# Down product of a gated FFN: five places for raw operands in place of three, and three work lists reordered

## What is computed

```
h = rms_norm(x, norm_ffn)
up = causal_dwconv(h @ ffn_w_up, ffn_conv_w, ffn_conv_b)        # 2048 x 5632, three taps
u_val, u_gate = split(up, 2)
x = x + (gelu(u_gate) * u_val) @ ffn_w_down                     # 2816 -> 1024
out = rms_norm(x, norm_final)
```

## Time and profile before

| | us |
|---|---|
| median of 3 runs (lowest, highest) | 2575.82 (2570.79, 2579.19) |
| the profiled execution | 2580.78 |
| its span in the trace | 2579.0 |
| down product of half 0, first matmul to first matmul of what follows three uses later | 1664.55 to 1912.53 |
| down product of half 1 | 2341.34 to 2560.31 |
| TensorE busy | 2435.2 (94%) |

### The profile page before, as it was taken

How to read it: one execution, slowest core, us unless ns; L and a number is a source line. 1 busy time by engine, 2 the same in 40 slices (tenths; PEclk the granted TensorE clock), 3 DMA queues, 4 the chain that set the end, 5 groups by cost and what they waited for, 6 DMA issues and landing times.

```text
span 2579.0 us, 33398 instructions
## 1 busy us (share of the span) xinstructions
PE 2435.2 (94%) x11968; PEld 1952.1 (76%) x11968; DVE 1707.7 (66%) x2323; ACT 1129.5 (44%) x2008; POOL 978.5 (38%) x784
## 2 busy tenths in 40 slices
PE   7999999999799996997899999999899999998997
PEld 5777777777677775775688888777678788787886
DVE  7554447775255675351787887767778888886755
ACT  6434254332146554321544444443564444444444
POOL 4111003432055772221555555333235556551310
PEclk9999999899899998998899999999999999999999
DMA  4233324442497424544332332386542322326764
GB/s 163 98 98 103 100 74 152 142 150 93 157 312 247 129 63 163 178 157 172 151 116 100 114 116 98 119 277 225 188 155 95 119 102 106 119 90 211 234 193 161
DMA packets 189444, 376.60 MB, mean 146 GB/s; under 512 B 17104, under 2 KB 61152, under 8 KB 180192
## 3 DMA queue, kind: packets, MB, share of 16 engines
q1 hardware_dynamic: 189280, 374.47, 42.7%
HBM read 250.43 MB, written 123.98 MB: 145 GB/s over the span
## 4 chain that ended last, share of the span: by engine, by line
PE 38%; DVE 7%; issue 2%; DMA 2%; ACT 2%; POOL 1%; SPq 0%; ACTq 0%; DVEq 0%; POOLq 0%
PE ff_bank L2107 13%; PE ff_bank L2109 12%; PE ff_bank L2108 12%; DVE ff_ring L2817 2%; DVE ff_y_gate L2804 2%; DMA ff_raw_ring<-t_t 1%; DVE ff_ring L2765 1%; DVE ff_b_lo L2759 1%; ACT ff_y_gate L2619 1%; DMA ff_raw_ring<-a_t 0%; ACT ff_ring L2634 0%; DMA ff_b_raw<-h_t 0%; DVE ff_u L2786 0%; ACT ff_e L2598 0%; DVE ff_u L2788 0%
## 5 line engine op out<-in xcount | busy, mean ns | idle before, releaser
L2107 PE MATMUL ff_bank<-ff_b_hi,ff_ring 128*128 128x512 f32 x1232 | 486.6, 395 | 29.7 <-DVE ff_b_lo L2759 13.0
L2108 PE MATMUL ff_bank<-ff_b_lo,ff_ring 128*128 128x512 f32 x1232 | 482.3, 392 | 0.0
L2109 PE MATMUL ff_bank<-ff_b_hi,ff_ring 128*128 128x512 f32 x1232 | 482.2, 391 | 0.0
L2817 DVE TENSOR_TENSOR ff_ring<-ff_raw_ring,ff_ring 128x512 fp32r<-128x512 f32 x308 | 240.2, 827 | 132.9 <-ACT ff_ring L2634 132.8
L66 PE MATMUL ip_bank<-ip_x_hi,ip_w_hi 128*128 128x512 f32 x736 | 306.1, 416 | 20.0 <-DVE ip_x_lo L701 16.8
L2107 PEld LDWEIGHTS ff_bank<-ff_b_hi,ff_ring 128*128 128x128 f32 x1232 | 232.8, 189 | 93.7 <-issue 43.2
L67 PE MATMUL ip_bank<-ip_x_lo,ip_w_hi 128*128 128x512 f32 x736 | 296.8, 403 | 0.0
L68 PE MATMUL ip_bank<-ip_x_hi,ip_w_lo 128*128 128x512 f32 x736 | 295.9, 402 | 0.0
L2107 PE MATMUL ff_bank<-ff_ring 128*128 128x512 f32 x616 | 245.2, 398 | 27.5 <-DVE ff_ring L2817 23.4
L2109 PEld LDWEIGHTS ff_bank<-ff_b_hi,ff_ring 128*128 128x128 f32 x1232 | 232.9, 189 | 49.2
L2108 PEld LDWEIGHTS ff_bank<-ff_b_lo,ff_ring 128*128 128x128 f32 x1232 | 233.1, 189 | 47.8 <-issue 0.5
(11 more groups left out here) (263 smaller groups left out, 4618.4 us busy)
## 6 DMA issues: line engine op xcount, KB each, us to landing
ff_raw<-in_slabs SPq DMA_DIRECT2D x43, 1024.0 KB, 4.8
proj_t<-ip_staged SPq DMA_DIRECT2D x92, 256.0 KB, 2.7
a_t<-ff_y_val SPq DMA_DIRECT2D x44, 512.0 KB, 2.6
t_t<-ff_t_sum SPq DMA_DIRECT2D x88, 256.0 KB, 2.0
ff_raw_ring<-s_t SPq DMA_DIRECT2D x88, 256.0 KB, 3.2
ff_raw_ring<-t_t SPq DMA_DIRECT2D x88, 256.0 KB, 3.8
ff_raw_ring<-in_w_down SPq DMA_DIRECT2D x66, 256.0 KB, 3.1
ff_raw_ring<-a_t SPq DMA_DIRECT2D x66, 256.0 KB, 4.4
```

What stands on the lines that cost most here:

```text
L2107: pe.matmul(out, w_hi, x_hi, start=first, stop=False, skip_group_check=resumed)
L2108: pe.matmul(out, w_hi, x_lo, start=False, stop=False, skip_group_check=resumed)
L2109: return pe.matmul(out, w_lo, x_hi, start=False, stop=last, skip_group_check=resumed)
L2817: dve.tensor_tensor(ring[:, to, 1, :], raw_ring[:, raw_slot(half, n), i, :], ring[:, to, 0, :].bitcast(F32), ALU.subtract).then_inc(d_lo_r ...
```

## The change

Two more raw places, `spare`, are put over `b_hi[6]`. Steps take places by n mod 5; in half 0 only up to step 64, from step 65 they take the old three again, and `high_b` of B11 waits until the low parts of step 64 are made. A load waits for the low parts of the last step that had its place; loads 3 and 4 wait for the end of the half's up product, since they go where `b_hi[6]` was. Lists: on SyncE the last stores go from behind load 8 to behind load 10, `load_x` to behind 14 to 29, `load_piece` to behind 30 to 45. On ScalarE high step 3 goes ahead of the last tap; squares go to 56 to 59 and 62 to 65, `high_b` starts at 48. On VectorE low step 3 goes ahead of the last convolution and low step 4 between it and the gating; `norm_b` comes one per step from 36 to 51. On GpSimd the last four totals of half 0 go ahead of the sums of the next slab.

```diff
+        spare = placed("spare", [P, 2, 2, KH * P], 6 * KH * NB * 4)
-        d_in = [sem(f"d_in{i}") for i in range(3)]
+        d_in = [sem(f"d_in{i}") for i in range(5)]
+        RAW_FIVE = 65
-        def raw_slot(half, n):
-            return slot(half, n % 3)
+        def raw_number(half, n):
+            return n % 5 if half or n < RAW_FIVE else (n - RAW_FIVE) % 3
+        def raw_at(half, n, i):
+            r = raw_number(half, n)
+            return raw_ring[:, slot(half, r), i, :] if r < 3 else spare[:, r - 3, i, :]
+        def raw_before(half, n):
+            return [m for m in range(n) if raw_number(half, m) == raw_number(half, n)][-1]
...
-                if n >= 3:
-                    sp.wait_ge(d_lo_ready, 2 * (N - 2))
-                else:
-                    sp.wait_ge(product_done, USES * half + 146)
+                if n >= 5:
+                    sp.wait_ge(d_lo_ready, 2 * (STEPS * half + raw_before(half, n) + 1))
+                else:
+                    sp.wait_ge(product_done, USES * half + (146 if n < 3 else USES))
...
-                    if n == 8:
+                    if n == 10:
                         store_a(half, PAIRS - 1)
                         store_t(half, PAIRS - 1)
-                    if 10 <= n < 26:
-                        load_x(half, n - 10)
-                    if half == 0 and 26 <= n < 42:
-                        load_piece(1, n - 26)
+                    if 14 <= n < 30:
+                        load_x(half, n - 14)
+                    if half == 0 and 30 <= n < 46:
+                        load_piece(1, n - 30)
...
                 totals(half, range(OC, 3 * OC))
                 if half == 0:
+                    totals(half, range(3 * OC, 4 * OC))
                     last_sum_of_slab(1, 0)
                     sums_of_slab(1, 1)
-                if half == 0:
-                    totals(half, range(3 * OC, 4 * OC))
...
+                    if o == B11:
+                        act.wait_ge(d_lo_ready, 2 * RAW_FIVE)
...
                 high_step(half, 2)
+                high_step(half, 3)
                 tap(half, PAIRS - 1, 0)
-                for n in range(3, STEPS):
+                for n in range(4, STEPS):
-                    if 44 <= n < 48:
-                        square(half, n - 44)
-                    if 60 <= n < 64:
-                        square(half, n - 60 + OC)
+                    if 56 <= n < 60:
+                        square(half, n - 56)
+                    if 62 <= n < 66:
+                        square(half, n - 62 + OC)
...
-                    if half == 0 and 46 <= n < 46 + 28:
-                        high_b(1, n - 46)
+                    if half == 0 and 48 <= n < 48 + 28:
+                        high_b(1, n - 48)
...
                 low_step(half, 2)
+                low_step(half, 3)
                 convolve(half, PAIRS - 1, 0)
+                low_step(half, 4)
                 multiply(half, PAIRS - 1)
-                for n in range(3, STEPS):
+                for n in range(5, STEPS):
-                    if half == 0 and 33 <= n < 49 and n % 4 == 1:
-                        for i in range(4):
-                            norm_b(n - 33 + i)
+                    if half == 0 and 36 <= n < 52:
+                        norm_b(n - 36)
```

More of the change, by code:

```diff
@@ L2264, in loads_of @@
         def loads_of(half, n):
-            return n // 3 + 1 + half * len(range(n % 3, STEPS, 3))
+            r = raw_number(half, n)
+            return len([0 for h in range(half + 1) for m in range(STEPS if h < half else n + 1) if raw_number(h, m) == r])
         def down_count(half, n, o):
@@ L2354, in load_step @@
                     w = s_t[i, :, SUM_AT[weights], :]
-                sp.dma_start(raw_ring[:, raw_slot(half, n), 1, :], w).then_inc(d_in[n % 3], 16)
+                sp.dma_start(raw_at(half, n, 1), w).then_inc(d_in[raw_number(half, n)], 16)
                 if acts[0] == "B":
@@ L2363, in load_step @@
                     a = t_t[t, i, :, half * NB:(half + 1) * NB]
-                sp.dma_start(raw_ring[:, raw_slot(half, n), 0, :], a).then_inc(d_in[n % 3], 16)
+                sp.dma_start(raw_at(half, n, 0), a).then_inc(d_in[raw_number(half, n)], 16)
             def load_x(half, i):
@@ L2627, in high_step @@
                 N = STEPS * half + n
-                act.wait_ge(d_in[n % 3], 32 * loads_of(half, n))
+                act.wait_ge(d_in[raw_number(half, n)], 32 * loads_of(half, n))
                 if n >= 4:
@@ L2633, in high_step @@
                 for i, to in enumerate((act_slot(half, n), weight_slot(half, n))):
-                    act.activation(ring[:, to, 0, :], raw_ring[:, raw_slot(half, n), i, :], ACT.Copy).then_inc(d_hi_ready, 1)
+                    act.activation(ring[:, to, 0, :], raw_at(half, n, i), ACT.Copy).then_inc(d_hi_ready, 1)
             def keep_first_product(half):
@@ L2816, in low_step @@
                     dve.wait_ge(d_hi_ready, 2 * N + i + 1)
-                    dve.tensor_tensor(ring[:, to, 1, :], raw_ring[:, raw_slot(half, n), i, :], ring[:, to, 0, :].bitcast(F32),
+                    dve.tensor_tensor(ring[:, to, 1, :], raw_at(half, n, i), ring[:, to, 0, :].bitcast(F32),
                                       ALU.subtract).then_inc(d_lo_ready, 1)
```

## The result

| | before | changed |
|---|---|---|
| median (lowest to highest), 4 runs each | 2574.38 (2570.79 to 2579.19) | 2543.75 (2540.20 to 2549.77) |
| ratio, 95% interval | | 0.9877 (0.9859 to 0.9895) |
| the profiled execution | 2580.78 | 2542.92 |
| first down matmul of half 0 | 1664.55 | 1656.60 |
| half 0, to the last matmul before the squares' sum | 248.0 | 226.4 |

30.6 us came off the median; 35.7 were forecast. Between the two profiled executions lie 37.9 us, but 8.0 of them stand ahead of the first down matmul, where nothing was changed.

A forecast was written before the change was run, and what follows sets the result against it. TensorE, kept waiting in places, was taken to bound the kernel. Gains 9.6 + 4.35 + 16.3 + 5.5 = 35.7 us brought the profiled 2580.8 to 2545.1, or 2540.1 us for a median; range 2529 to 2559.

The forecast's parts named there:

- A, the head: Start of both halves' down products: earlier high and low steps remove most of the wait at step 3; 9.6 us gained.
- B, the copy: First product's copy, both halves: loads 11 to 14 go out ahead of the store wait, no wait left; 4.35 us gained.
- C, the middle: Middle of half 0: later squares free ScalarE, norms are spread; 5.0 us of loss left, 16.3 us gained.
- D, the border: Border of half 0 to half 1: earlier totals cut the squares' sum wait from 5.3 to 1.5 us; 5.5 us gained.
- the two bounds: At the head, load 3's activation block lands 3.1 or 4.9 us after it goes out.
- The rival of late loads: Load 3 lands 6 us after issue, TensorE waits at steps 3 to 5, A gives nothing; 2550 us, chance 0.08.
- The lag sum: Middle of half 0: VectorE's lag from norms, sums, drain and `low_b` stalls TensorE 3.9 us at step 52 or 53.
- The dearer price in the prediction: Middle of half 0: each GpSimd sum costs VectorE its full length less idle time, near 1.3 us; 3 us more stall.

The follow-up runs named there:

- lists alone: The changed kernel with the old three raw places instead of five, its reordered lists kept; 2561.0 us, ratio to before 0.9940.
- the memsets: The changed kernel with GpSimd's sixteen sums of normed operands replaced by memsets of the same tiles; 2541.4 us, one run.
- the norms at 33: The changed kernel with VectorE's norms one per step from 33 to 48 instead of 36 to 51; 2543.5 us, ratio to before 0.9855.
- the squares at 50: The changed kernel with the first four squares before high steps 50 to 53 instead of 56 to 59; 2553.0 us, one run.
- the totals late: GpSimd's last four totals behind the slab sums, as before the change; the changed kernel with only this undone took 2542.4 us.
- the old order at the head: The changed kernel with high step 3 and low steps 3 and 4 back behind tap, convolution and gating; 2555.7 us, ratio to before 0.9919.
- the slab sum first: The changed kernel with GpSimd's last sum of slab (1, 0) ahead of the last four totals; 2548.9 us.

## Why the prediction was right

The four terms, in us of the stages, from the tables above:

| term | forecast | measured |
|---|---|---|
| A, the head | 9.6 | 8.7 |
| B, the copy | 4.35 | 4.6 |
| C, the middle | 16.3 | 14.8 |
| D, the border | 5.5 | 1.9 |
| all stages | 35.7 | 29.9 |

**A, the head: 9.6 us forecast, 8.7 measured** (12.9 us lost before, 4.2 after; undoing the order alone costs 8.5). Load 3 landed within the two bounds (1657.17 to about 1661.1 us, 3.9 against 3.1 to 4.9). The stall came in three small pieces a half, not two, without a clock drop: 1.0 and 1.2 us idle, 2.0 and 2.2 us lost against the 1.8 forecast. The rival of late loads is out.

**B, the copy: 4.35 forecast, all gained.** The reason stood too narrowly. I gave the depth and the later residual loads one sentence; lists alone show that the later loads are not enough, and that without the depth they double the price.

**C, the middle: 5.0 us left forecast, 6.1 left.** Of these 3.5 are the two waits, 0.6 the pick-up behind them, 1.6 lie in matmuls that start 0.43 us apart after the second wait, and 0.3 are near step 58. The clock in 2.5 us stretches (length, busy PE, PEld, DVE, ACT, POOL, clock, DMA share, GB/s):

```profile
1804.50:1807.00 2.50, 0.48 (x2) 0.27 (x2) 2.50 (x3) 2.19 (x4) 2.50 (x2) 1.00 0.20 75
1807.00:1809.50 2.50, 2.50 (x8) 1.98 (x8) 2.50 (x3) 0.00 (x1) 1.68 (x2) 0.61 0.62 170
```

The lag sum put 3.9 us at step 52 or 53; measured were 3.5 idle, at steps 52 and 53. The dearer price in the prediction, each sum at its whole length, would have left 8; 6.1 lies between the two and does not decide. That the middle's loss comes from GpSimd's sums beside VectorE is shown by the memsets, though not how much of it is their reading and how much their length; the lag sum itself is borne out by the norms at 33, not shown term by term. That squares held ScalarE, and ScalarE TensorE, is shown by the squares at 50.

**D, the border: 5.5 forecast, 1.9 measured.** This step failed, and it is most of the difference between 35.7 and 29.9. Even 1.9 is generous: the three kernels with the totals late have 428.4 to 428.8 us there, the eight with the changed order and no other edit at the border 426.9 to 427.8. The prediction said that the slab sums end 6 us later and are "wanted for use 8, TensorE being there at 1928". TensorE was not the first to want them: ScalarE was, with the high part of use 8 ahead of the root in its list. ScalarE stood 3.36 us there, the copy for use 11 came 1.7 us later for it, and TensorE paid 2.65 us at use 11. The rest of these 2.65 us is a second thing the prediction left out: the path from the squares' sum to that copy takes 23.6 us even when nothing holds it up, and a TensorE that waits less at the sum, and keeps its clock, reaches the end of that path too early. I had followed the moved step's data to TensorE, not through the list of the engine in between.

The range (2529 to 2559) held both medians of the changed kernel, 2543.8 and 2548.4. They lie 3.7 and 8.3 us above the forecast; D's 3.6 us, C's 1.5 and A's 0.9 are of that size. The range is as wide as the gain itself and would have held the median with D worth nothing, so it does not vouch for D.

## What to carry to other kernels

In a pipeline of fixed lists, more buffers remove waits for data (83.3 us of ScalarE's with three places and new lists, 5.8 in the changed kernel) and moved list entries remove waits for order. Price them apart and place by place: at the head only the order counted, at the copy only the depth, in the middle they overlapped, and the two totals added up only by chance. A wait that is shortened also lets its engine arrive sooner at the next one: ask what has slack there. When a step is moved later, look for the first instruction in any list that waits for it, and for what stands behind that one, and not only for the engine that needs the value. Reorder a low part or a copy that frees a buffer only after asking which load waits for it: 8 us later there became 11 us of waiting for ScalarE and 5.6 us for the stages.

## What was not expected of the hardware

In the changed kernel a wait of 2.02 us, shorter than the 2.45 and 2.65 us ones behind which the clock stayed at 1.00, was followed by 0.61 in the next 2.5 us stretch; 1.46 us of idling lay 5 us ahead of it. But the kernel with the old order at the head has the same pair, 1.46 and 2.06 us, and kept 1.00:

```profile
1815.00:1817.50 2.50, 2.50 (x11) 2.06 (x12) 2.50 (x2) 0.21 (x1) 1.96 (x2) 1.00 0.60 141
```

So neither the length of the last wait nor that of the two together decides, and what does is open.

Four GpSimd memsets ran beside two low parts without slowing either, where four subtractions made each low part wait about 1 us. And it is not always VectorE that stands. In half 1 of the kernel with the slab sum first, six low parts ran at their own pace and one GpSimd subtraction took 5.89 us; SyncE's store of its result, at 2330.93, confirms that length. In the kernel with the old order at the head two of GpSimd's totals took 8.99 us, while VectorE's low parts of that time took 0.6 us each:

```profile
1836.62 8.99 POOL L2530 TENSOR_TENSOR ffn_rstd<-ffn_rstd,ff_squares 128x512 f32<-128x512 f32 x2 [3.78 <-ACT ff_squares L2665]
...
1837.52 1.28 DVE L2831 TENSOR_TENSOR ff_ring<-ff_raw_ring,ff_ring 128x512 fp32r<-128x512 f32 x2
```
